# State products of a gated recurrence: row tiles, column count and the layout of the values

## The reference, cut to what matters

```python
ds = jnp.einsum('bnshk,bnshv->bnhkv', k * jnp.exp(last[:, :, None] - cum), v)

def step(s, inp):
    dec, d = inp
    return dec[..., None] * s + d, s

s_fin, s_start = lax.scan(step, s0, (jnp.moveaxis(jnp.exp(last), 1, 0), jnp.moveaxis(ds, 1, 0)))
o_inter = jnp.einsum('bnthk,nbhkv->bnthv', q * jnp.exp(cum), s_start)
```

## Time and profile before

| | |
|---|---|
| median of 3 runs | 1770.18 us (1768.29 to 1771.09) |
| the profiled execution | 1766.58 us |
| its span in the trace | 1764.8 us |
| TensorE busy | 1619.8 us, 92% of the span |
| VectorE, ScalarE, GpSimd busy | 518.8, 429.1, 219.9 us |
| mean granted clock of TensorE | 0.967 of full speed |

### The profile page before, as it was taken

The page is one execution under the profiler, slowest core; times in us unless marked ns, Lnnn a source line. Parts: engine busy times, 40 slices in busy tenths (PEclk is TensorE's granted clock), DMA queues, the critical chain, the costliest instruction groups (busy, mean ns, idle before and its releaser), DMA issues. The chain is left out here.

```text
span 1764.8 us, 26274 instructions
## 1 busy us (share of the span) xinstructions
PE 1619.8 (92%) x9008; PEld 1016.0 (58%) x9008; DVE 518.8 (29%) x1309; ACT 429.1 (24%) x943; POOL 219.9 (12%) x182
## 2 busy tenths in 40 slices
PE   6999989999999997898889999899999998878887
PEld 3665556655676554455466656566558655555555
DVE  2055654411124111111141556542111431111113
ACT  3144224510122111111132342353001311111110
POOL 0003200000002133232100022000000022232220
PEclk8999999999998999999999999899999899999999
DMA  9512234452336999999982024326132299999993
GB/s 360 205 58 96 64 136 160 160 173 96 143 117 255 335 382 390 359 365 394 347 323 88 25 96 99 117 83 204 48 143 96 102 358 361 389 370 360 386 369 128
DMA packets 166113, 385.82 MB, mean 219 GB/s; under 512 B 21020, under 2 KB 58908, under 8 KB 165536
## 3 DMA queue, kind: packets, MB, share of 16 engines
q1 hardware_dynamic: 140976, 340.28, 52.1%
q0 software_dynamic: 16992, 24.96, 5.8%
q10 hardware_dynamic: 8016, 18.90, 2.9%
HBM read 372.27 MB, written 31.98 MB: 229 GB/s over the span
## 5 line engine op out<-in xcount | busy, mean ns | idle before, releaser
L786 PE MATMUL ab<-hT,slot 128*128 128x384 f32 x1344 | 452.8, 492 | 10.5 <-PEq L814 6.3
L786 PEld LDWEIGHTS ab<-hT,slot 128*128 128x128 f32 x1344 | 256.1, 192 | 194.3 <-issue 26.3
L786 PE MATMUL vb<-slot,arena 128*64 128x256 f32 x2560 | 307.2, 395 | 62.9 <-PEq L836 62.8
L786 PEld LDWEIGHTS vb<-slot,arena 128*64 128x64 f32 x2560 | 205.1, 142 | 147.9 <-issue 84.3
L688 POOL DMA_INDIRECT expert_sums<-arena,sum_index x72 | 112.9, 1568 | 362.2 <-POOLq L687 178.9
L2096 DVE SCALAR_TENSOR_TENSOR arena<-vb,unit_gate,arena 128x128 f32<-128x128 f32 x80 | 28.1, 351 | 386.4 <-DVEq L2095 386.4
L786 PE MATMUL ab<-slot,hT 128*128 128x384 f32 (+1 forms) x384 | 118.1, 463 | 0.0
L1540 ACT ACTIVATE arena<-vb 128x128 f32<-128x128 f32 x92 | 25.5, 278 | 362.0 <-ACTq L1539 362.0
L786 PE MATMUL vb<-nat,arena 128*64 128x512 f32 (+1 forms) x480 | 109.5, 535 | 1.8 <-PEq L954 1.2
L820 PEld LDWEIGHTS ab<-con,arena 128*128 128x128 f32 x532 | 60.2, 145 | 80.4 <-issue 79.1
L1411 ACT ACTIVATE con<-ab,sm 128x384 f32<-128x384 f32 x64 | 37.3, 582 | 277.2 <-ACTq L1309 277.1
(11 more groups left out here) (269 smaller groups left out, 1519.7 us busy)
## 6 DMA issues: line engine op xcount, KB each, us to landing
slot<-in_w_up SPq DMA_DIRECT2D x64, 2048.0 KB
slot<-in_w_mod SPq DMA_DIRECT2D x24, 2048.0 KB
slot<-in_w_mgate SPq DMA_DIRECT2D x32, 1024.0 KB
nat<-in_w_down SPq DMA_DIRECT2D x32, 1024.0 KB, 18.2
slot<-in_w_in SPq DMA_DIRECT2D x10, 2048.0 KB
arena<-in_w_down SPq DMA_DIRECT2D x16, 1024.0 KB, 19.3
hT<-in_w_down SPq DMA_DIRECT2D x16, 1024.0 KB, 20.1
slot<-in_w_out SPq DMA_DIRECT2D x4, 2048.0 KB
```

The source lines that it names most:

```text
L786: i = nc.tensor.matmul(out, lhsT, rhs, start=start, stop=stop, skip_group_check=True)
```

## The change

Half the tokens of a tile belong to chunks 0 to 3 (partitions 0 to 63), half to chunks 4 to 7 (partitions 64 to 127). The changed kernel multiplies the two halves apart, as two row tiles of 64 tokens, and stores chunk `c` and chunk `c+4` in the same 64 columns of `VX`, each on its own partitions.

- ScalarE makes four spread copies a tile instead of eight. The scale is a new small tile `half_chunk`, the sum of columns `c` and `c+4` of `chunk`, which VectorE computes once a layer.
- TensorE runs eight matmuls a round (two pairs, two row tiles, two heads) of 64 rows, 64 columns and 256 moving columns, instead of four of 128 rows, 64 columns and 512 moving columns. A bank now holds one row tile with both pairs, instead of one pair with all chunks. Both banks are waited for ahead of the first matmul.
- VectorE reads the same 64 columns per step from another place. ScalarE's wait for the constants goes, since it no longer reads `chunk`.

```diff
+        half_chunk = small[:, 52:56]
...
                     for t in ((0, 1, 2), (0, 2, 1))[r]:
                         pe.wait_ge(vx_ready, 1).then_inc(vx_ready, -1)
+                        banks = pair_of_banks()
                         for pr in range(2):
-                            def ds(o):
+                            for rt in range(2):
+                                rows = slice(64 * rt, 64 * rt + 64)
                                 for h2 in range(2):
                                     h = 2 * pr + h2
-                                    last = mm(o[64 * h2:64 * h2 + 64, :], kdN[:, t, 64 * h:64 * h + 64], VX[:, h, :],
-                                              True, True)
-                                return last
-                            group(v, ds)
+                                    last = mm(vb[banks[rt]][64 * h2:64 * h2 + 64, 256 * pr:256 * pr + 256],
+                                              kdN[rows, t, 64 * h:64 * h + 64], VX[rows, h, 0:256], True, True, True)
+                                if pr == 1:
+                                    last.then_inc(vfull[banks[rt]], 1)
...
-                        elif l == 0 and r == 0:
-                            act.wait_ge(con_in, 16)
-                        for c in range(TC):
+                        for c in range(TC // 2):
                             f(VX[:, :, HD * c:HD * c + HD], nat[:, t, 0:4 * HD].rearrange("p (h v) -> p h v", v=HD),
-                              ACT.Identity, scale=c_("chunk")[:, c:c + 1])
+                              ACT.Identity, scale=half_chunk[:, c:c + 1])
...
+                vec.tensor_tensor(half_chunk, c_("chunk")[:, 0:TC // 2], c_("chunk")[:, TC // 2:TC], ALU.add)
...
-                            for pr, b in ((0, b0), (1, b1)):
+                            for pr in range(2):
+                                b = b0 if c < TC // 2 else b1
+                                at = 256 * pr + HD * (c % (TC // 2))
...
-                                    vb[b][:, HD * c:HD * c + HD], ALU.mult, ALU.add)
+                                    vb[b][:, at:at + HD], ALU.mult, ALU.add)
```

More of the change, by code:

```diff
@@ L929, in _, with pair_of_banks @@
                 for r in range(2):
+                    def pair_of_banks():
+                        banks = [v.next(), v.next()]
+                        for b in banks:
+                            pe.wait_ge(vfree[b], 1).then_inc(vfree[b], -1)
+                        return banks
                     late = EARLY + LATE * r
```

## The result

The changed kernel takes 1757.32 us (median of 4 runs, 1755.15 to 1760.63), the kernel before beside it 1769.54 us: a ratio of 0.9929, 95% interval 0.991 to 0.9948. The forecast was 1760.5 us, 3.2 us above the new median; the median lies inside the forecast's range of 1756 to 1766, 1.3 us from its lower end. The profiled execution took 1755.15 us, its span is 1753.3 us. It was 2.2 us faster than the median; the profiled one of before was 3.6 us faster than its own.

What follows compares the result with a forecast made beforehand. TensorE was taken to bound the recurrence: 10.1 us saved over twelve rounds less 0.4 us for VectorE's added wait gave 9.7 us, from the median 1770.2 to 1760.5 us. The 8-in-10 range was 1756 to 1766 us.

Steps and rivals of the forecast that it cites:

- What bounds the kernel: Recurrence: TensorE runs nearly without a gap, so time taken from its stream there is taken from the end.
- The round: TensorE's state products, twelve rounds: four records abreast, 1.03 us instead of 1.87, 10.1 us saved in all.
- the 64*32 products: Recurrence's output products, 64 rows by 32 columns: 32 records in 0.60 us, read as eight abreast.
- The edges: First load and changes to and from the projection's shape around a TensorE round: 0.15 us, no dearer than now.
- The second wait: VectorE before the scan: one more wait, about 0.1 us, exposed once a direction, 0.4 us lost; bounds 0 and 1.0.
- sum of 9.7 us: Whole saving: 10.1 us from TensorE's rounds less 0.4 us for VectorE's added wait.
- The second bank's wait on TensorE: Now before a round's first product; costs nothing, since the scan of two rounds ago frees the bank in time.
- Does it reach the end?: Behind the recurrence: the expert stage starts earlier by what was saved, 4.8 us a layer; first expert transfer near 539.
- Rival 3: Gained but partly given back, by clock stages or a held expert stage: half the gain, 1765.3 us; chance 0.05.
- The clock: Granted clock in shifted stages may fall otherwise, 2 to 3 us either way; stays 1.00 in the recurrence.
- Rival 1: State products run only two abreast: rounds of 1.91 us, 1771.1 us, no change that can be told; chance 0.07.
- Rival 2: State products run one at a time: rounds of 3.7 us, 1792 us; chance 0.04.

Runs made afterwards that it cites:

- e2: Changed kernel, but ScalarE makes eight spread copies a tile again, the extra four to columns nothing reads; ratio 0.9942 to the kernel before.
- e3: Changed kernel, but both row tiles use the rows of tokens 0 to 63, products of tokens 64 to 127 left out; ratio 1.0003 to the kernel before.
- e5: Changed kernel with the row tile as outer loop of a round's sixteen records; one run, 1757.51 us.
- e4: Changed kernel taken further: four row tiles of 32 tokens, 128 columns, four banks, two spread copies; ratio 0.9942 to the kernel before.
- e8: Changed kernel, but only a round's last product signals and VectorE waits once instead of twice; ratio 0.9936 to the kernel before.
- e7: Changed kernel with four row tiles, VectorE's four waits spread over the scan's first steps, banks freed as the scan passes; ratio 0.9928 to the kernel before.
- e6: Changed kernel, but VectorE's second bank wait and its signal to ScalarE moved behind the scan's first step; ratio 0.9938 to the kernel before.
- e9: Changed kernel with four row tiles, one signal and wait a round, banks freed as scanned and requested in that order; 1755.73 us, ratio 0.9935 to before.
- e1: Changed kernel again, unchanged, five rounds; 1760.49 us beside 1767.15 for the kernel before, ratio 0.9955.
- e10: Changed kernel once more, unchanged, on the same chip as e11; 1755.39 us, ratio 0.9929 to the kernel before.
- e11: The kernel of e9 once more, on the same chip as e10; 1754.92 us, ratio 0.9922 to the kernel before.

## Why the prediction was right, step by step

**What bounds the kernel.** Right. TensorE's stream is the time of the recurrence: twelve rounds shorter by 0.84 us make 10.1 us, and 9.2 us came out of the two stretches. With ScalarE's work doubled again (e2) the stretches didn't move.

**The round.** 1.03 us forecast, 1.03 measured. The reading that carried it was the one on the 64*32 products. e3 shows that the two row halves side by side are the cause and not the smaller records, their number or the copies, and e5 that it isn't their order. (Which rows of the array work and which partitions are read go together in all these runs; none parts the two.) The estimate of 1.15 us a round from the Trainium skill (page "TensorE: Matmul & The Clock Gate", section "Measured speedup vs the span model") was too dear, and it left out the edges of 0.15 us that the measured 1.03 includes. The four steps that e3 adds cost 0.21 us each, and the step read from the expert stage was 0.22, so four places lose nothing that can be seen against two; and in e4, with four row tiles times two columns, 32 records took 0.62 us, about as long as the 32 records of the 64*32 products.

**The edges** stayed what they were: 0.15 us taken, 0.19 by e3's sum with a step of 0.21.

**The second wait.** The condition and the size were right: 0.1 us at each of the four last states, 0.4 us in all, since the scan starts 0.36 us behind the round instead of 0.25, and it is 0.25 again in e3, where the banks don't fill together. That the time is VectorE's wait itself and not the second signal is argued, not shown; e8, which drops both, gets 0.08 back. The idle times grew by more than that: from the third block's start to the last state TensorE has 5.61, 5.54, 5.54 and 5.60 us before (the earlier trace rows show the first and the last) and 5.84, 5.63, 5.63 and 5.98 after, 0.8 us more in all. The other 0.4 us are longer scans, which the sum had not: in the first direction the last scan takes 4.50 us instead of 4.36, and in the last one it breaks off for 0.43 us (shown below). In layer 0 another 0.1 us is lost in the products behind the last state. So the sum of 9.7 us was 0.5 too high, inside its bounds of 8.5 to 11.2. The lower bound isn't worked out there: its dearest price for the wait, 1.0 us, gives 10.1 - 1.0 = 9.1, and 9.2 is just above that. Two of the four idle times, 0.41 and 0.56 us, lie outside the 0.2 to 0.3 that were to show it right.

**The second bank's wait on TensorE, the new sum, ScalarE's dropped wait at nothing.** Right: TensorE has no idle time ahead of any round. e4 and e7 show the condition that was put on it: with all four banks in use, TensorE stood 0.1 to 0.6 us ahead of rounds.

**Does it reach the end?** Yes. SyncE's first expert transfer, which answers to the earlier trace rows:

```profile
541.24 0.45 SPq L562 DMA_DIRECT2D slot<-in_w_up  x1
```

It is issued at 541.24 instead of 543.77; "near 539" was forecast. The first round started 5.4 us later than before, so the recurrence of layer 0 ended later too, at 193.93 instead of 193.17, where "some 5 us earlier" was forecast. Counted from the first round the transfer comes 7.9 us earlier (429.02 instead of 436.93), of which 4.6 are the recurrence. Rival 3 has nothing for it: over three comparisons 19 runs of the changed kernel have a mean of 1758.4 us and 35 of the kernel before 1768.4, 10.0 us with a standard error of about 0.9 (12.0, 7.9 and 12.3 in the three).

**The clock.** 2 to 3 us either way was forecast; it is more. The first 60 us alone run at 0.77 to 0.89 in thirteen profiles of nearly the same instructions, and the first round then starts between 113.5 and 106.8, in step with it (table above): at 107.4 in e6 and 107.6 in e9, which have the change, and at 112 in e1, which has it too. In the recurrences it was 1.00 in every trace.

The clock of each run is on record, and it explains about half of the scatter: over 132 runs of nine kernels (the one before, the changed one and seven of the experiments), with one slope for all, a run is 1.0 us longer for each 0.001 of mean granted clock that it lacks, and the scatter of 3.3 us a run falls to 2.3. With that slope taken out, which makes the figures estimates, the changed kernel is 9.3 us faster than the one before (standard error 0.6), e3 0.1 us slower (0.8) and e9 14.8 us faster (0.7); the stretches of their traces say 9.2 us faster, 0.5 slower and 13.6 faster. In e1, which gave the smallest difference, the changed kernel's mean clock was 0.001 below that of the kernel before beside it, and in e10 0.003 above.

So the saving was forecast by its mechanism, 9.7 us against 9.2. That the measured median came 3.2 us from the forecast and inside the range is partly luck: the first part of the profiled execution lost 5.4 us and the two later ones won 7.7.

**The rivals.** Rival 1 (two abreast) is what e3 brings about: 1.87 us a round and a ratio of 1.0003, so its price was right, and the changed kernel is not it. Rival 2 has no sign in any run. e4 is the lesson on the other side: the same step taken once more had four fifths of its gain missing, and got it back in e9 with one signal, one wait and the banks in the reader's order.

## What to carry to other kernels

When a small product leaves part of the array unused, row tiles and column tiles can multiply, as they did here for float32 products on four and eight places, and the price can be read from a product of the same kernel that is packed that way. Every row tile had its own bank here; no run tried it otherwise. After a producer gets shorter, look at the chain that starts at its end: signal once, wait once, free buffers as the reader passes them and ask for them in that order. An effect under 1% that sits in one stage is measured by that stage's landmarks in the trace, since the stages around it can scatter by as much as the effect.

## What the runs showed of the hardware

Each signal of TensorE with its wait of VectorE cost 0.08 us in the chain when the banks fill together: the scan starts 0.28 us behind the round with one and 0.36 with two (two row tiles, e8 and the changed kernel), 0.31 with one and 0.55 with four (four row tiles, e9 and e4). With the banks full two steps apart the second one cost nothing that can be seen (0.25 us in e3).

A scan breaks off for 0.43 us at one or two places, the same places in every trace of a kernel: ahead of the last step of the last scan in the changed kernel (three traces) and in e2, e3, e5 and e6, elsewhere too or instead in e4, e7, e8 and e9, and nowhere in the kernel before. VectorE's timeline of the changed kernel:

```profile
1044.33 3.75 DVE L1774 SCALAR_TENSOR_TENSOR arena<-arena,small,vb 128x64 f32<-128x64 f32 x14 [2.09 <-DVEq L1766]
1048.51 0.47 DVE L1774 SCALAR_TENSOR_TENSOR arena<-arena,small,vb 128x64 f32<-128x64 f32 x2 [0.43 <-issue]
```

and its transfers from 1046 to 1050 (GB/s in 40 slices of 0.1 us, then the queue with its packets, MB and share):

```profile
GB/s 0 0 0 0 0 0 0 0 0 0 0 0 0 0 0 0 0 0 0 0 0 0 0 0 0 0 0 0 0 0 0 0 82 0 0 0 0 0 0 0
...
q14 instruction: 1, 0.01, 0.6%
```

The same break in e9, in layer 0:

```profile
120.58 3.88 DVE L1774 SCALAR_TENSOR_TENSOR arena<-arena,small,vb 128x64 f32<-128x64 f32 x14 [1.55 <-DVEq L1766]
124.90 0.47 DVE L1774 SCALAR_TENSOR_TENSOR arena<-arena,small,vb 128x64 f32<-128x64 f32 x2 [0.43 <-issue]
```

In six such pauses (the changed kernel, e4, e7, e8, e9, e11), 0.43 to 0.48 us long, one packet of an instruction queue follows 0.6 to 0.7 us behind the pause's end, and in e3 0.93 us behind it; in the changed kernel the pause ends at 1048.51 and the packet comes at 1049.2. The Trainium skill (page "Runtime: NRT & Kernel Launch", section "Instruction fetch mechanics") has each engine's instructions brought in blocks by its own DMA queue, at a cost that is mostly hidden. A pause that moves with the code and has such a packet beside it fits that, and where VectorE is waited for, the 0.43 us are not hidden. That the packet belongs to the pause was not tried, and stays open.
